# Hybrid attention decode step: small steps moved between the page steps, the pool-state stores and row reloads moved behind the last page requests

## The reference, cut to what matters

```
h = RMSNorm_pre(x);  z = h @ W_in               # q k v qi ki wi ga xb gb u vc gc
A: indexer scores -> top-k mask -> softmax attention over K/V (prompt: new keys; sample: paged cache)
B: pooling mixer: trailing means over xb and a state of 15 earlier rows, then pool_w, pool_scale
C: gating unit: u * (tril(W_s) @ layernorm(vc) + b)
y = concat(A*silu(ga), B*silu(gb), C*silu(gc)) @ W_out;  x = x + RMSNorm_post(y)
```

## Time and profile before

| | |
|---|---|
| median of 3 runs | 1002.05 us (999.57 to 1002.63) |
| the profiled execution's own time | 999.5 us |
| its span | 997.8 us |
| mean granted clock of TensorE | 0.994 |
| PE busy | 934.6 us (94%) |
| DVE / ACT / POOL busy | 54% / 31% / 27% |

### The profile page before, as it was taken

One profiled execution on the slowest core, in us unless ns is written; L12 is line 12 of the kernel. 1 busy time (PEld: TensorE's weight loads), 2 busy tenths in 40 slices (PEclk: granted clock), 3 DMA queues, 4 the chain that ended last, 5 costly groups with the idle time before them and its releaser, 6 DMA issues.

```text
span 997.8 us, 20531 instructions
## 1 busy us (share of the span) xinstructions
PE 934.6 (94%) x7100; PEld 483.7 (48%) x7100; DVE 535.9 (54%) x1718; ACT 305.4 (31%) x674; POOL 272.6 (27%) x484
## 2 busy tenths in 40 slices
PE   5798999999999999998999999999999999999996
PEld 3434444444454555554555444444445455555543
DVE  4336999475883233233444499966678623332232
ACT  3121121432124245423231211225212424543312
POOL 8710232232222211413342013223222222241110
PEclk9899999999999999999999999999999999999998
DMA  9841677576866655856584338766677667566551
GB/s 314 166 134 43 211 265 250 187 245 226 295 212 212 240 191 186 305 165 222 149 246 128 110 105 280 249 226 207 244 262 246 198 214 249 167 229 247 170 179 53
DMA packets 91954, 205.21 MB, mean 206 GB/s; under 512 B 15047, under 2 KB 26550, under 8 KB 91858
## 3 DMA queue, kind: packets, MB, share of 16 engines
q0 software_dynamic: 38944, 123.98, 36.5%
q1 hardware_dynamic: 47778, 75.78, 23.2%
q10 hardware_dynamic: 5136, 4.20, 1.5%
HBM read 193.88 MB, written 10.14 MB: 204 GB/s over the span
## 4 chain that ended last, share of the span: by engine, by line
PE 74%; DMA 8%; ACT 5%; DVE 4%; issue 4%; ACTq 3%; SPq 1%; POOL 0%; POOLq 0%; DVEq 0%
PE bank L1490 36%; PE bank L1847 10%; PE bank L1507 5%; PE bank L1542 5%; DMA pg<-in_cache_k_dram 4%; PE bank L1473 4%; ACTq L624 2%; PE bank L1723 2%; DMA pg<-in_cache_v_dram 2%; PE bank L1759 2%; PE bank L1591 2%; DMA r<-in_x_prompt_dram 2%; PE bank L1649 1%; PE bank L1565 1%; DVE r L1399 1%
## 5 line engine op out<-in xcount | busy, mean ns | idle before, releaser
L1490 PE MATMUL bank<-wr,ht 128*128 128x512 f32 (+1 forms) x1024 | 436.2, 579 | 5.3 <-DVE ht L1198 2.0
L1490 PEld LDWEIGHTS bank<-wr,ht 128*128 128x128 f32 x1024 | 190.8, 191 | 219.2 <-issue 202.7
L705 POOL DMA_DIRECT2D wr<-in_w_in_dram x50 | 37.1, 742 | 293.0 <-PE bank L1490 225.2
L722 POOL DMA_DIRECT2D pg<-in_cache_v_dram x128 | 69.8, 546 | 165.1 <-PE bank L1542 121.3
L722 POOL DMA_DIRECT2D pg<-in_cache_k_dram x128 | 69.5, 543 | 83.3 <-PE bank L1507 59.2
L1116 DVE TENSOR_SCALAR_CACHE_REDUCE r<-r,sel_i 128x1088 bf16<-128x1088 f32 x62 | 82.8, 1336 | 0.0
L1507 PE MATMUL bank<-pg,qbx 128*32 128x256 f32 x1024 | 63.4, 383 | 7.6 <-DMA pg<-in_cache_k_dram 4.2
L1473 PE MATMUL bank<-wr,ht 128*32 128x256 f32 (+1 forms) x1152 | 65.2, 379 | 2.9 <-DMA wr<-in_w_in_dram 2.6
L1542 PE MATMUL bank<-pg,rs 128*32 128x256 f32 x1024 | 62.3, 382 | 1.8 <-DMA pg<-in_cache_v_dram 1.8
L1847 PE MATMUL bank<-wr,qt 128*128 128x512 f32 x128 | 58.4, 599 | 1.8 <-ACT rs L923 1.8
L1847 PE MATMUL bank<-wr,ht 128*128 128x512 f32 x128 | 57.5, 592 | 0.0
(11 more groups left out here) (271 smaller groups left out, 1167.3 us busy)
## 6 DMA issues: line engine op xcount, KB each, us to landing
pg<-in_cache_k_dram SPq DMA_DIRECT2D x128, 256.0 KB, 5.0
pg<-in_cache_k_dram POOLq DMA_DIRECT2D x128, 256.0 KB, 5.8
pg<-in_cache_v_dram SPq DMA_DIRECT2D x128, 256.0 KB, 5.0
pg<-in_cache_v_dram POOLq DMA_DIRECT2D x128, 256.0 KB, 5.8
wr<-in_w_in_dram POOLq DMA_DIRECT2D x40, 512.0 KB, 4.2
wr<-in_w_in_dram POOLq DMA_DIRECT2D x6, 1024.0 KB, 6.0
wr<-in_w_in_dram POOLq DMA_DIRECT2D x2, 2048.0 KB, 16.6
wr<-in_w_out_dram POOLq DMA_DIRECT2D x8, 512.0 KB, 4.1
```

The source lines that it names most:

```text
L705: pool.dma_start(W[n % 2][:, k, d0:d0 + w], src[k.start * P:k.stop * P, c0:c0 + w].rearrange("(k p) n -> p k n", p=P))\
L722: pool.dma_start(PG[2 * gi + e], cache[l, bass.ds(nos[2 * gi + e], 1), :, :].rearrange("o p n -> p (o n)"))\
L1490: mm = pe.matmul(b[0:m, 0:w], HT[:, k, rt * P:rt * P + m], W[n % 2][:, k, 0:w], start=(k == 0), stop=(k == KC - 1))
```

## The change

Five things are moved; nothing is added or taken away, and SP's list is the same.

1. `T qi 2` and `T qi 3` come one slot later (slots 11 and 12 in place of 10 and 11).
2. `pi 3 3` goes from the end of slot 23 to behind `K 2 0` in slot 24; `yo 0` and `yo 1` go one slot later.
3. `L 1 3` (slot 33) and `L 3 0` (slot 38) go behind the page step of their slot.
4. The eight stores of the pool's state are issued at the step `yT ST` (slot 45) in place of `z xg ST` (slot 39).
5. `ldsmall` and the reloads `xl` go from slot 43 to slot 44, the reloads ahead of `ldsmall`.

```
-PI_PLACES = [(n, part) for n in (18, 19, 20, 21, 22, 23) for part in (1, 3)]
+PI_PLACES = [(n, part) for n in (18, 19, 20, 21, 22) for part in (1, 3)] + [(23, 1), (24, 3)]
...
     for rt in range(PT_TILES):
-        put(at["qi", rt] + 1, FRONT, ("T", "qi", rt))
+        put(at["qi", rt] + 1 + (rt >= 2), FRONT, ("T", "qi", rt))
...
     for m, ((i, c), n) in enumerate(zip(HPAIRS, heads)):
-        put(n, ROWS_A, ("L", i, c))
+        put(n, ROWS_B if n in (33, 38) else ROWS_A, ("L", i, c))
...
                     put(n, COLS, ("V", p, NCH), ("od", p))
-                    put(n + 1, FRONT, ("yo", p))
+                    put(n + 1 + (p < 2), FRONT, ("yo", p))
...
-    put(43, BACK, ("ldsmall",), ("xl", ST), ("xl", 2), ("xl", 3))
+    put(44, BACK, ("xl", 2), ("xl", ST), ("xl", 3), ("ldsmall",))
...
-                elif kind == "z" and s[2:] == ("xg", ST):
-                    pool.wait_ge(act_free, act_emptied(*s))
+                elif kind == "yT" and s[2] == ST:
+                    pool.wait_ge(act_free, act_emptied("z", l, "xg", ST))
                     for b in range(NB):
                         pool.dma_start(pool_sample[l, b, NSTATE - TQ:NSTATE, :],
                                        ZA[b * TQ:(b + 1) * TQ, ST, 0:DP]).then_inc(st_xb, 16)
```

## The result

| | before | changed kernel |
|---|---|---|
| median | 1002.26 us (4 runs, 999.57 to 1002.63) | 1018.13 us (4 runs, 1013.76 to 1024.56) |
| ratio, 95% interval | | 1.0169 [1.0112, 1.0227] |
| profiled execution, its span | 999.5, 997.8 us | 1018.34, 1016.6 us |
| mean granted clock of TensorE | 0.994 | 0.983 |

The change makes the kernel 1.7% slower. The page's part 1 of the changed kernel answers to the earlier trace rows; the columns are the same.

What follows compares the result with a forecast made beforehand. The prediction took the kernel as bound by PE's own list, busy 934.6 of 997.8 us. It summed 999.5 + 18.8 + 1.9 − 0.5 − 0.1 − 1.7 = 1017.9, added 1.1 and said 1019 us, range 1012 to 1027.

Steps and rivals of the forecast that it cites:

- the queue-bound landing: Layer 0's late stores land 4 to 7 us after the last is issued, giving 1015 to 1024 us; chance 0.72.
- The stall, 18.8 us: ACT's Square of norm 1 0 waits for the late stores until 484.0, starting 18.8 us late and stalling PE before out 2 0.
- The clock, 1.9 us: After PE's idle time before out 2 0, its clock runs at half speed for 3.9 us, losing 1.9 us.
- Stores and loads of layer 1 and the loads of layer 0, 0 us: Layer 1's stores and reloads, and layer 0's reloads and small weights, hold up nothing in their new places: 0 us.
- `V 2 3`, -0.5 us: With the stores no longer ahead of the page requests for V 2 3 in slot 39, 0.5 us is won.
- `pi 3 3` and `yo 0`, -0.1 us: In layer 0 a new wait of about 1.0 us before K 2 0 replaces 1.08 before K 2 1: sum -0.1 us.
- `L 1 3` and `yo 1`, -1.7 us: A longer interval before K 3 1 wins 0.76 us in layer 0 and about 0.9 in layer 1: -1.7 us.
- `L 3 0`, 0: The sample tile still hides the time from L 3 0 to the transposes that need it, by 0.3 us: 0.
- `T qi`, 0: Moving T qi 2 and T qi 3 near K 0 1 brings 0, with -0.5 to +0.8 us per layer.
- the short landing (1.7 us): The queue is empty when layer 0's late stores are issued, so they land in 1.7 us: 1014.3 us; chance 0.14.
- The long one (12.4 us): Layer 0's late stores take 12.4 us to land, as the sample stores had before: 1025 us; chance 0.08.
- The case on the other side: The Square's wait for stores is hidden and page waits win: 997.2 us, down to 993.5; chance 0.05.

Runs made afterwards that it cites:

- experiments 1 to 3: Changed kernel with sample stores put back: 0.9959; kernel before with only those stores moved: 1.0206; changed kernel with the Square waiting for the prompt's store alone: 0.9947.
- experiment 3: Changed kernel, stores still late, prompt's store on its own semaphore and the Square of norm 1 0 waiting for that alone: 997.86 us, ratio 0.9947.
- the small steps together: Kernel before with only items 1 to 3 of the change moved; stores, reloads and small weights as before: 999.97 us, ratio 0.9962.
- experiment 4, first run: Changed kernel with sample stores issued at V 3 2, right behind the page requests for V 3 3, ahead of reloads and small weights: 1011.79 us, ratio 1.0074.
- experiment 1: Changed kernel with the eight sample stores back at the tile of slot 39, all other moves kept: 999.38 us, ratio 0.9959.

## Why the prediction was right, point by point

The prediction was 1019 us, within 1012 to 1027; the result is 1018.13 us, and the likeliest case, the queue-bound landing, is the one that came.

*The stall, 18.8 us.* Measured against the start of `V 3 2` on PE in each trace: 482.91 - 463.54 = 19.4 us after it, where it was 465.19 - 463.99 = 1.2 before, so 18.2 us late. It is shown by experiments 1 to 3 that this wait is the loss. The last store landed 4.6 us after its issue at 478.3 where the sum had 5.3, and two terms within that were off in opposite ways: the eleven DMAs were through at 474.3 + 7.1 = 481.4 and not at 483.3, and the last store landed 1.5 us behind them and not 0.7. The reloads took longer to land than before, 8.8 to 10.6 us against 7.3 to 9.6. The estimate of about 1 us for the missing second copy of rows to `x_mid` fits experiment 3: there the copy goes out at 474.35, and the stores land 5.9 to 6.6 us after their issue, against 4.4 to 6.0 without it.

The Trainium skill's rule for one DMA (DMA: Bandwidth & Descriptors, "Anatomy of one DMA") would have had the last store down 2.0 us after its issue, by estimate. The measured landing of these eight was 4.4 to 6.0 us, and 3.7 to 5.0 us with the reloads behind them. The windows of the changed kernel (columns as above) split the 4.6 us of the last one:

```profile
480.60:480.80 0.20, 0.00 (x0) 0.00 (x0) 0.00 (x0) 0.00 (x0) 0.00 (x0) 0.50 0.13 16
```

```profile
481.00:482.00 1.00, 0.00 (x0) 0.00 (x0) 0.00 (x0) 0.00 (x0) 0.00 (x0) 0.50 0.00 0
```

The core's DMA traffic ended by about 480.8, 2.5 us after the issue, and the Square started 2.1 us after that, with the DMA share at nothing. So the second part is near the rule's fixed 2.0 us, and what the rule leaves out is the queue ahead.

*The clock, 1.9 us.* Measured 2.4: the first half of `out 2 0` took 6.11 us and not 3.70. The windows of the changed kernel, with the columns as above, against the earlier trace rows:

```profile
469.00:470.00 1.00, 0.00 (x0) 0.00 (x0) 0.00 (x0) 0.00 (x0) 1.00 (x3) 1.00 0.67 180
470.00:471.00 1.00, 0.00 (x0) 0.00 (x0) 0.00 (x0) 0.00 (x0) 0.29 (x1) 0.79 0.99 354
471.00:472.00 1.00, 0.00 (x0) 0.00 (x0) 0.00 (x0) 0.00 (x0) 0.56 (x1) 0.50 1.08 430
...
490.00:491.00 1.00, 1.00 (x2) 0.42 (x2) 0.00 (x0) 0.00 (x0) 0.00 (x0) 0.50 0.00 0
491.00:492.00 1.00, 1.00 (x3) 0.38 (x2) 0.00 (x0) 0.00 (x0) 0.00 (x0) 0.97 0.00 0
```

The clock came back 4.8 us after PE's first product, not 3.9. Half of 4.8 is 2.4: the mechanism was right, and the time at half speed was the term off.

*Stores and loads of layer 1 and the loads of layer 0, 0 us.* Right. The last store of layer 1 was issued at 974.8 and landed at most 11.0 us later, 31 us before the span ended, and the loads moved alone give 1.0005 [0.9987, 1.0023].

*`V 2 3`, -0.5 us.* Its wait in layer 0 is gone in the changed kernel, as said, but the reason given is not borne out. The wait was put down to the stores ahead of the requests, and the six other traces with the stores in slot 39 name no such wait either. It was a wait of one execution, not the price of the stores.

*`pi 3 3` and `yo 0`, -0.1 us.* This is the step that failed. The wait of 1.08 us before `K 2 1` went as said, but the wait of about 1.0 us before `K 2 0` that was to take its place did not come. The sum took the landing of the earlier trace rows, 7.5 us for the last page, as given. In that trace nothing hung on it, since the page was in time. In the seven traces with these steps moved the longest landing was 5.9 to 7.4 us (6.4 in the changed kernel). In five of them `K 2 0` has no wait; after 7.0 us (the small steps together) it waits 0.24 us, and after 7.4 (experiment 4, first run) 0.62. So the mechanism is there at the long end, and the size failed: one landing of one execution was taken for what the next would be. The view of line 722 in the changed kernel, 237 to 240 us, against the earlier trace rows:

```profile
L722 POOL DMA_DIRECT2D pg<-in_cache_k_dram x4: 537/538/539, 237.6 to 239.4; - x4
...
DMA to landing us min/median/max: 4.2/5.5/6.4
```

*`L 1 3` and `yo 1`, -1.7 us.* Measured -2.3 with an interval of 2 us to either side; the wait in layer 0 is gone, that in layer 1 fell from 1.8 us to 0.4, by 1.4 and not by 0.9. *`L 3 0`, 0.* Right: no wait before `P 3 0` in the timeline of PE, in the changed kernel or with this part alone. *`T qi`, 0.* The time is not told from none, 0.9989 [0.9974, 1.0005]; the waits at `K 0 1` to `K 0 3` hint that it was more than nothing.

In the profiled execution the page waits fell by 3.6 us where the prediction had 2.3; 1.0 us of the difference is the wait before `K 2 0` that did not come. So the sum came out near its execution (1017.9 against 1018.34 us) partly because errors met: the stall 0.6 us too high and the gains 1.3 too small, the clock 0.5 too low and the 1.4 us of clock at the early tile not in it. That they met is luck. The rivals: of the short landing (1.7 us) the condition came half true, since the DMA engines were through by 480.8 and not 483, but it is ruled out by the shortest landing of the eight, 4.4 us. The long one (12.4 us) is ruled out by the longest, 6.0 us, and by experiment 4, whose stores stood right behind 2 MB of pages and still landed within 5.0 us. The case on the other side, no wait and a small gain, is what experiments 1 and 3 then made real.

What stays open is why the sample stores of the kernel before took 10.1 to 12.4 us: their place, behind 2 MB of weights and ahead of the pages, was not tried apart. In the three other kernels with `L 3 0` in its old place they took 9.9 to 12.2 us there, and in the three in which `L 3 0` had moved 8.1 to 10.3. Open too is what decides, after a wait of 2 us or so, whether the clock falls.

## What to carry to other kernels

Before a DMA is moved later in a queue, look up every wait on the semaphore it counts on, and not only the reader of its data: a sum over several transfers makes each waiter wait for the last of them, needed or not. Here one counter stood for nine stores of which the waiting instruction needed one, and giving that one a counter of its own took the changed kernel from 1.0169 to 0.9947 of the kernel before, some 22 us, and made the late stores free. Price a stall on TensorE as its length plus the clock. And look at the granted clock before a difference of 1 or 2 us between two traces is put down to the change.

## What the runs showed of the hardware

A short wait can cost more in clock than in time, and its length alone does not tell whether it will. The first half of `out 2 0` shows it. With 1.52 and 1.62 us idle before it, it took 3.70 us; with 1.83 us it took 3.70 in five traces and 5.39 in a sixth; with 2.94 us it took 5.40; with 12.91, 5.68; with 19.98, 6.11; with 20.66, 5.90. So a fall of the clock cost 1.7 to 2.4 us here, nearly whatever the length of the idle time. In the case of 2.94 us PE had stopped at 466.6 and the clock fell in the stretch 470 to 471, when PE was at work again. The early tile says the same: after waits of 2.5 to 2.6 us it took 3.66 us in five traces, and after waits of 2.5 to 2.8 us 5.0 to 5.4 in seven.

Such falls are part of why runs of one kernel differ. With the stores put back (experiment 1), the twelve runs go from 993.22 us at a mean granted clock of 0.994 to 1004.02 us at 0.989.

Eight stores of 8 KB landed 3.7 to 5.0 us after issue right behind 2 MB of pages, 4.4 to 6.0 us behind the reloads and small weights, 5.9 to 6.6 us there with a copy of 512 KB beside them, 9.4 to 11.0 us in layer 1 of the same changed kernel, and 8.1 to 12.4 us in their old place, over seven kernels. For the last store of the changed kernel 2.1 us of it passed after the core's last DMA traffic. One figure for a small DMA does not exist here; the nearest row from the same queue state was the best guide.
